# Issuing the small products beside an input projection as interleaved 64-row tiles of the TensorE array

## The reference, cut to what matters

```python
w_log = -softplus(-(w0 + tanh(zw) @ w_decay_up)) - 0.5      # decay: 64 rows of contraction
a = sigmoid(a0 + za @ w_a_up)                               # 64 rows of contraction
kk = kk / maximum(sqrt(sum(kk * kk, -1)), 1e-12)            # sum over each head of 64
bonus = sum(r * k * r_k, -1) * v                            # sum over each head of 64
gate_r = sigmoid(einsum('btni,nij->btnj', xb, w_rg) + b_rg) # 8 blocks of 64 x 64
gate_i = sigmoid(einsum('btni,nij->btnj', xb, w_ig) + b_ig) # 8 blocks of 64 x 64
```

## Time and profile before

| | |
|---|---|
| median of 3 runs | 1851.29 us (1848.05 to 1852.13) |
| span of the profiled execution | 1850.6 us, 21482 instructions |
| mean granted TensorE clock in it | 0.902 of full speed |
| TensorE matmul busy | 1477.0 us (80%), 8153 instructions |
| VectorE busy | 1159.3 us (63%), 1167 instructions |
| ScalarE busy | 806.0 us (44%), 866 instructions |
| GpSimd busy | 469.0 us (25%), 343 instructions |

### The profile page before, as it was taken

The page is one execution under the profiler, slowest core; times in us unless marked ns, Lnnn a source line. Parts: engine busy times, 40 slices in busy tenths (PEclk is TensorE's granted clock), DMA queues, the critical chain, the costliest instruction groups (busy, mean ns, idle before and its releaser), DMA issues.

```text
span 1850.6 us, 21482 instructions
## 1 busy us (share of the span) xinstructions
PE 1477.0 (80%) x8153; PEld 934.3 (50%) x8202; DVE 1159.3 (63%) x1167; ACT 806.0 (44%) x866; POOL 469.0 (25%) x343
## 2 busy tenths in 40 slices
PE   3899899949999999977999229998998899899700
PEld 2565555539999999841454214444444444444300
DVE  6346466655555555424497818778777777877566
ACT  7265533323333333336000316765566566656310
POOL 4400211132222222100654341122112211211075
PEclk9999999969999999986999559999999999989955
DMA  7621111000000000030211458989898898988372
GB/s 207 222 75 42 54 45 35 23 1 1 1 0 0 0 0 0 0 143 1 95 57 46 194 153 335 373 331 372 360 363 343 356 378 353 352 358 361 133 271 95
DMA packets 74639, 302.08 MB, mean 163 GB/s; under 512 B 18128, under 2 KB 40672, under 8 KB 62288
## 3 DMA queue, kind: packets, MB, share of 16 engines
q1 hardware_dynamic: 56976, 239.03, 34.4%
q0 software_dynamic: 17600, 62.20, 8.7%
HBM read 261.33 MB, written 39.88 MB: 163 GB/s over the span
## 4 chain that ended last, share of the span: by engine, by line
PE 45%; DVE 25%; ACT 13%; issue 10%; POOL 4%; DMA 2%; DVEq 0%; POOLq 0%; ACTq 0%; SPq 0%
PE ps L1622 12%; DVE big L1161 7%; PE ps L1591 7%; PE ps L1789 6%; ACT big L1463 6%; PE ps L1815 4%; PE ps L1817 4%; PE ps L1814 4%; PE ps L1628 3%; DVE big L923 3%; PE ps L1611 2%; POOL scr_tok L690 1%; DVE big L1184 1%; DVE big L1176 1%; ACT big L1382 1%
## 5 line engine op out<-in xcount | busy, mean ns | idle before, releaser
L1161 DVE TENSOR_TENSOR big<-big 128x4096 bf16<-128x4096 f32 x96 | 424.1, 4421 | 137.8 <-ACT big L1463 137.8
L1463 ACT ACTIVATE big<-big 128x4096 bf16<-128x4096 f32 x96 | 347.1, 3620 | 224.4 <-PE ps L1817 219.8
L1815 PE MATMUL ps<-big 128*128 128x512 bf16 x768 | 309.0, 402 | 35.9 <-DVE big L1176 31.5
L1814 PE MATMUL ps<-big 128*128 128x512 bf16 x722 | 289.3, 401 | 33.5 <-DVE big L1176 33.5
L1622 PE MATMUL ps<-big 128*128 128x128 f32 x2176 | 272.0, 280 | 17.5 <-DVE big L923 5.7
L1622 PEld LDWEIGHTS ps<-big 128*128 128x128 f32 x2176 | 256.1, 192 | 30.6 <-DVE big L923 9.5
L1591 PE MATMUL ps<-big 128*128 128x347 f16 (+1 forms) x1656 | 255.5, 316 | 16.1 <-DVE big L790 11.3
L1591 PEld LDWEIGHTS ps<-big 128*128 128x128 f16 (+1 forms) x1656 | 163.3, 99 | 111.1 <-issue 16.2
L1817 PE MATMUL ps<-big 128*128 128x512 bf16 x765 | 201.2, 400 | 0.2
L1375 ACT ACTIVATE big<-ps 128x512 f32<-128x512 f32 (+2 forms) x119 | 63.0, 568 | 251.1 <-PE ps L1628 167.8
L1814 PEld LDWEIGHTS ps<-big 128*128 128x128 bf16 x768 | 77.8, 101 | 171.5 <-DVE big L1176 76.5
(11 more groups left out here) (270 smaller groups left out, 1673.0 us busy)
## 6 DMA issues: line engine op xcount, KB each, us to landing
big<-in_w_exp_gate_dram SPq DMA_DIRECT2D x32, 2048.0 KB, 10.2
big<-in_w_exp_up_dram SPq DMA_DIRECT2D x32, 2048.0 KB, 9.2
big<-in_w_exp_down_dram SPq DMA_DIRECT2D x32, 2048.0 KB
scr_y<-big POOLq DMA_DIRECT2D x32, 512.0 KB, 8.3
big<-in_w_in_dram SPq DMA_DIRECT2D x22, 512.0 KB, 3.7
scr_h<-big POOLq DMA_DIRECT2D x16, 512.0 KB, 4.1
scr_y<-big POOLq DMA_DIRECT2D x1, 8192.0 KB, 26.1
big<-scr_h SPq DMA_DIRECT2D x16, 512.0 KB, 4.1
```

The source lines that it names most:

```text
L1161: v.tensor_tensor(wsp[s][k][1], raw[k], wsp[s][k][0], ALU.subtract).then_inc(s_lo[k], 1)
L1463: f(wsp[s][k][0], raw[k], ACT.Copy).then_inc(s_hi[k], 1)
L1814: mm(out_, x[0][:, k, :], w[0][:, k, cs], start=k == 0, stop=False)
L1815: mm(out_, x[0][:, k, :], w[1][:, k, cs], start=False, stop=False)
```

## The change

The small jobs are issued in another way. "gr" and "gi" become one call, `gate_pair`: every product of 128 x 128 is split in its two diagonal blocks of 64 x 64, and a block of "gr" on one half of the partitions alternates with a block of "gi" on the other half; each job now has six matmuls of 64 rows and 64 columns for the three of before. "dec" and "aa" become one call, `decay_pair`: the same three matmuls each, alternating between the two halves of the rows. "ss" and "bon" are issued by `head_sums` as six matmuls of 64 x 64 each, alternating between the halves, and writing different segments at a time.

A pair writes both sets of banks, so it waits on the read-out of the job just before it (n-1) too. Both jobs of a pair are signalled by their last matmuls at the end of the pair, and ScalarE and VectorE wait, for the first job of a pair, on the count of its mate (`done`). VectorE also waits on a second semaphore, `s_half`, for the sums over heads. The order of the list, the projection jobs and the work of the other engines stay.

```diff
+        s_half = sem("s_half")
         SHIFTED = [j for j in JOBS if j[0] in ("z", "r", "k", "v")]
+        MATE = {"gr": "gi", "dec": "aa"}
+
+        def done(job):
+
+            kind, j = job
+            return J[(MATE.get(kind, kind), j)] + 1
...
-                    dv.wait_ge(s_job, jb[("ss", p)] + 1)
+                    dv.wait_ge(s_job, done(("ss", p)))
+                    dv.wait_ge(s_half, 2 * p + 1)
...
-                    dv.wait_ge(s_job, jb[("bon", p)] + 1)
+                    dv.wait_ge(s_job, done(("bon", p)))
+                    dv.wait_ge(s_half, 2 * p + 2)
...
-                ac.wait_ge(s_job, J[job] + 1)
+                ac.wait_ge(s_job, done(job))
...
+            halves_ = [slice(0, HEAD), slice(HEAD, P)]
+
+            def gate_pair(n, j):
+
+                pe.wait_ge(s_gate_w, 64)
+                pe.wait_ge(LRU_D.sem, LRU_D.at(j, "c3"))
+                last = {}
+                for flip in range(2):
+                    for q in range(3):
+                        for k, (kind, w) in enumerate((("gr", wrg), ("gi", wig))):
+                            h = k ^ flip
+                            rws = halves_[h]
+                            last[kind] = mm(bank((kind, j))[rws, q, :], w[rws, j, rws], XC[rws, q * SEG:(q + 1) * SEG],
+                                            start=True, stop=True)
+                last["gr"].then_inc(s_job, 1)
+                last["gi"].then_inc(s_job, 1)
+
+            def decay_pair(n, j):
+
+                pe.wait_ge(s_zact, 1)
+                pe.wait_ge(s_prm, 16 * 16)
+                last = {}
+                for q in range(3):
+                    for kind, rws in (("dec", halves_[0]), ("aa", halves_[1])):
+                        last[kind] = mm(bank((kind, j))[:, q, :], wlr[rws, j * P:(j + 1) * P],
+                                        Z0[rws, q * SEG:(q + 1) * SEG], start=True, stop=True)
+                last["dec"].then_inc(s_job, 1)
+                last["aa"].then_inc(s_job, 1)
+
+            def head_sums(n, kind, j):
+
+                if kind == "ss":
+                    pe.wait_ge(PR_A.sem, PR_A.at(j, "sq"))
+                    pe.wait_ge(s_const_done, 1)
+                else:
+                    pe.wait_ge(PR_D.sem, PR_D.at(j, "q"))
+                for q in range(3):
+                    for h, rws in enumerate(halves_):
+                        seg = (q + 2 * h) % 3
+                        last = mm(bank((kind, j))[rws, seg, :], blk[rws, h, :], T7[rws, seg * SEG:(seg + 1) * SEG],
+                                  start=True, stop=True)
+                        if q == 2 and h == 0:
+                            last.then_inc(s_half, 1)
+                last.then_inc(s_job, 1)
+
             for n, job in enumerate(JOBS):
                 kind, j = job
+                if kind in ("gi", "aa"):
+                    continue
                 if n >= 2:
                     emptied(JOBS[n - 2])
+                if kind in MATE:
+                    emptied(JOBS[n - 1])
...
+                elif kind == "gr":
+                    gate_pair(n, j)
+                elif kind == "dec":
+                    decay_pair(n, j)
                 else:
...
-                    for q in range(3):
-                        last = mm(bank(job)[:, q, :], lhs, rhs[:, q * SEG:(q + 1) * SEG], start=True, stop=True)
-                last.then_inc(s_job, 1)
+                    head_sums(n, kind, j)
```

More of the change, by code:

```diff
@@ L864, in pair @@
             def pair(p, part):
-                jb = J
                 kt = KT[:, p, Q0:TP]
@@ L1592, in _ @@
                                           start=k == 0 and a_ == b_, stop=k == KD - 1 and a_ == 1)
-                else:
[L1594 to L1609, removed]
-                    for q in range(3):
-                        last = mm(bank(job)[:, q, :], lhs, rhs[:, q * SEG:(q + 1) * SEG], start=True, stop=True)
-                last.then_inc(s_job, 1)
+                    last.then_inc(s_job, 1)
+                elif kind == "gr":
+                    gate_pair(n, j)
+                elif kind == "dec":
+                    decay_pair(n, j)
+                else:
+                    head_sums(n, kind, j)
             def pair(m, p):
```

## The result

The changed kernel takes 1855.70 us, the median of 16 runs (1848.95 to 1871.58), beside 1850.39 us for the kernel before (16 runs, 1841.45 to 1853.39). The ratio is 1.0049 with a 95% interval of 1.0027 to 1.0071: slower by 9 us, where I had forecast 17 and a range that began at 1860. All ratios are of executions in the usual state; one of e11 (3914 us) and one of e12 (1877 us) ran in a slower one and are left out.

A forecast was written before the change was run, and what follows sets the result against it. In the gates TensorE and the ScalarE-VectorE-convolution chain tick nearly together; TensorE leads at p = 0 to 3. Gates 7.4, decay pairs 5.1, head sums 0.4 and half clock 4.2 us sum to 17.1: 1868.4 us, range 1860 to 1887.

The forecast's parts named there:

- Tiles side by side: Tiled products on different row halves overlap: decay pair 2.02 us, gate pair 3.74, head sum 2.02; chance 0.80.
- The rival of one after another: Tiles run one by one: gate pairs 7.2 us, decay pairs +1.7 each, total 1899; chance 0.12, whole or in part.
- Program order: Skill's rule taken literally: decay pair 0.3 us longer, gate pair 0.2, total 1870 where 1868 was given.
- Gate pair 0: First "gr"/"gi" pair waits for lx1's read-out, starts at 103.15; gl2 at 108.2, 3.2 us later.
- Gate pair 1: Second gate pair waits for ScalarE's weight half and lx copy, starting at 132.2 instead of 128.01.
- Pair 2: Third gate pair, after a turn of 29.1 us for 26.59, starts at 161.3, 6.7 us late; z0 at 166.4.
- z2: Projection job after the fourth gate pair: at 202.0, 9.1 us later than 192.91.
- pair 3: Fourth gate pair, starting at z1's read-out, 195.2: 5.6 us, the middle between full and half clock.
- Decay pairs: "dec" with "aa": v 5.47 us after k's end, where it was 4.17; 5.1 us lost over four.
- Half clock: Six new idle times ahead of pairs; half of them taken at 1.4 us each: 4.2 us, bounds 0 and 10.
- Sum: Whole loss: 7.4 + 5.1 + 0.4 + 4.2 = 17.1 us on the span of 1850.6.
- the last sentence of the first part: Nothing after the stage starts before it ends, so every us TensorE loses there on the path is lost at the end.

The follow-up runs named there:

- e11: Changed kernel with ScalarE copying a projection's result out before making the weight half; ratio 1.0007 (0.9983 to 1.0032).
- e12: Changed kernel, unchanged, measured and traced once more against the kernel before; ratio 1.0051 (1.0024 to 1.0079).
- e5: Kernel before with gates and head sums cut into alternating 64 x 64 tiles, no wait or signal moved between jobs; ratio 0.9974 (0.9950 to 0.9999).
- e16: Changed kernel, unchanged, traced once more for its expert loop: loop 646.3 us, recurrence's first step at 415.9 us.
- e4: Changed kernel's order, waits and signals with the products of the kernel before, full tiles, no interleaving; ratio 1.0126 (1.0093 to 1.0159).
- e6: Changed kernel with gates issued as before, decay pairs and tiled head sums kept; ratio 1.0008 (0.9985 to 1.0031).
- e10: Kernel before with ScalarE copying a projection's result out before making the weight half; ratio 0.9992 (0.9973 to 1.0010).

## Why the prediction was wrong, step by step

The direction and the mechanism were right, the size was not: 9 us by the first ratio (14 and 9 by the others) for 17 forecast, and a median below the range.

The stage itself, in the first trace of after:

- Tiles side by side: as said. A decay pair takes 2.03 us (2.02), a gate pair 3.72 (3.74), a head sum 1.97 (2.02). e5 shows that they cost nothing. The rival of one after another is out. Program order as the Trainium skill has it ("TensorE: Matmul & The Clock Gate", packing small matmuls: matmuls start and end in program order) would have given a decay pair 2.3 us by my reckoning, and this case's trace has 2.03. In the kernel before the order didn't hold either: at p = 3 the first record of "aa" starts at 362.62 us and the fifth of "dec", issued ahead of it, at 362.70. The same section says that matmuls on different row groups overlap, and there the trace agrees: the twelve records of the pair at 239.36 start in twos, 0.01 to 0.04 us apart.
- Gate pair 0: gl2 at 108.17, forecast 108.2. Gate pair 1 at 132.04, forecast 132.2. Pair 2 at 162.59 for 161.3, and z0 at 169.26 for 166.4: two stretches at half clock, 1.7 us each, which I had put in another term.
- z2 at 204.65 for 202.0, with pair 3 at 5.35 us (5.6 taken); z2 to k0 at 32.52 us (32.5).
- Decay pairs: v 5.45 us after the end of k (242.62 for 237.17), forecast 5.47; at p = 3 v is 14.9 us late (379.54), of which the pair's own is the 1.2 forecast.
- Half clock: two gate pairs (3.4 us together) and one decay pair with its projection (0.7 and 1.9 us). That is three of the six new idle times, as taken, and 6.0 us for the 4.2 of the sum. Two of the three "bon" of p = 0 to 2 were at full clock, though, 1.97 us for the 3.40 and 3.67 of the trace before, and gave 3 us back. I had kept all of them.
- Sum: 14.8 us later at the end of the stage, forecast 17.1. Over four traces of the changed kernel (417.4, 421.5, 422.6, 415.9) the mean is 419.4; over three of the kernel before (402.6, 401.6, 398.8) it is 401.0. That is 18.4 us, with single traces 13 to 24 us apart: the sum for the stage was good to 1.3, and 17.1 beside 14.8 says little.

**The step that failed** is the last sentence of the first part: "every us that TensorE loses here on the path is lost at the end". I took the 1446 us behind the stage as a constant, and added the stage's loss to the span of one execution. What was lost is 9, 14 and 9 us, and the intervals of the three ratios end at 13, 18 and 15 us, under the stage's 18.4. The recurrence is nearly a constant (699.6 and 699.3 us; 696 to 700 in the fifteen traces that have no delay of no use), the expert loop is not. It was 631 to 649 us long in eighteen traces, and in the sixteen without filling it was the shorter the more of it ran at full clock. The trace before gave the sign of it, had I looked: turns of 20.8 us at 0.92 granted beside turns of 19.1. A range for the whole needed some 8 us more on either side, and 1855.7 would have been in it. The loss of the stage stands. The first trace of the changed kernel was a lucky one: with a loop as long as in e16 its span would have been 1870. The median over sixteen executions isn't luck of that kind; part of the loss comes back in many of them, along with a higher mean granted clock. That this happens is measured, why it happens stays open.

## What to carry to other kernels

Pairing two jobs so that they run side by side doubles what must be free before either starts and delays the first result to the end of both: here the 2.0 us won per decay pair were already hidden behind a read-out, and the waits of 1.2 to 2.2 us on both sides of the pair were not. Interleave row tiles only where both outputs are already free, and let each job be read out by itself (the second half of this advice no run here tried). And before adding a stage's loss to the span, look whether what comes behind has one length or several. One trace can already show turns of two kinds; two traces may not show the scatter (3.3 us between the first two of the kernel before, 15 over four of the changed one).

## What the runs showed of the hardware

- Two tiles on different halves of the rows run side by side without stretching each other: the trace of after has two decay jobs of six records in 2.03 us, and its timeline has two records starting within the 0.2 us from 239.30 to 239.50:

```profile
239.36 0.56 PE L1610 MATMUL ps<-big 64*128 64x347 f32 x2 [2.20 <-ACT big L1338]
```

- They overlap even when one job is issued whole ahead of the other, but less: 2.69 us in e4 for 2.02 interleaved, both at full clock.
- After idle times of 2.2 us some pairs ran in part at half clock (1.2 GHz) and others not: two of three gate pairs (5.41 and 5.41 beside 3.72 us), one of three decay pairs in the first trace of after, three of three in e6.
- A VectorE operation over 1041 columns took 3.02 us beside a GpSimd one and 1.30 alone (e10).
- Filling TensorE's idle time in the expert loop raised its granted clock from 0.93 to 0.99 and left the time where it was (ratio 1.0001); TensorE then waited 26.1 us in all for gathered rows.
- The granted clock over the expert loop was 0.93 where the loop took 648 to 649 us and 0.96 to 0.97 where it took 631 to 633, in traces of the same loop code.
